# Attention stage of a two-layer diffusion block: row maxima in pairs, row sums by matmuls with ones, shift rows by one transposing matmul and DMA

## The chip, the cores and the metric

One core of one Trainium2 chip. The metric is the device time of one execution in microseconds; for each kernel the median of several runs is given.

## The reference

Two layers over 1024 latent and 256 context tokens of width 1024. Each layer projects the tokens into the features of three token mixers (grouped-query attention with 8 heads, latent attention with 4 heads, a gated linear recurrence), joins their outputs in one projection, and then runs a squared-ReLU MLP. The change touches only the softmax attention:

```python
s = jnp.einsum('bqhgd,bkhd->bhgqk', qi, k, preferred_element_type=F32) * scale
p = jax.nn.softmax(s, axis=-1).astype(v.dtype)
return jnp.einsum('bhgqk,bkhv->bqhgv', p, v)
```

Latent queries see all 1280 keys. Context queries see only the 256 context keys, and they are wanted in layer 0 alone.

## The kernel before, in words

The kernel is a row of stages (blocks), each of which ends with a barrier. `attention` (L1227) runs once in each layer, with the output projection behind it.

**Units and steps.** A unit is 512 queries of a pair of heads (`par` 0 and 1). A long unit goes over 10 key tiles of 128 keys in 10 steps; a short one (context queries, 2 steps) stands behind every fourth long one in layer 0. Layer 0 has 12 long and 3 short units (126 steps), layer 1 has 12 long ones (120 steps): 27 units in all. The first 8 long units of a layer belong to the grouped-query heads (called A here, tiles at_qq, at_qs, at_kk, at_ks, aq, av), the last 4 to the latent heads (B here, tiles qb, kb, bv).

**One step** on TensorE (`scores`, L1556): K·Q into a PSUM tile at_sT with the keys on the partitions, by 4 matmuls of 512 columns in A (2 per head, for the high and the low halves of the numbers) and 6 in B. ScalarE then takes exp of the 128x1024 tile (L1445) into a ring of PRING = 4 SBUF tiles at_p. Two steps later (LAG = 2) TensorE multiplies the values with at_p (`weighted`, L1568, fp32, the two heads into different halves of the output partitions) into at_acc, and GpSimd adds up at_p into at_accp (L1409, L1414: 9 additions in a long unit).

**Three small things** are needed around a unit, and all go through a ring of two one-bank PSUM tiles `sm` (at_small), in the order of one list, `small`. Task j writes sm[j % 2]; before it TensorE waits in `released` until task j - 2 has been read.
- *max*: the softmax shift must be known before the unit starts. So scores of 128 queries against up to 512 keys are computed once more with the queries on the partitions (L1511 in A, where the two heads use different halves of the input rows; L1515 in B), and VectorE takes the maximum along the row (L1465). A long unit has 24 of them (4 query tiles, key chunks of 512, 512 and 256, 2 heads), a short one 8. After the last of a unit VectorE combines the chunks (L1469) and negates (L1471).
- *row*: the shifts must be a row beside the query features, since the key side has a row of ones there. For each head four fp32 matmuls with one column of at_neg as weights and the identity moving (L1526, 16 instruction records per unit) make the row in PSUM, and ScalarE writes it to partition 64 of at_qs or 96 of qb (L1431).
- *sum* and *bc*: 8 fp32 matmuls with 128x128 of at_accp as weights and one column of ones moving (L1532, 16 records) give the row sums of a unit, VectorE takes 8 reciprocals per partition (L1475), and 8 fp32 matmuls against the identity (L1539, 16 records) spread them over the output layout. VectorE copies that to SBUF (L1480) and multiplies at_acc with it (L1483); ScalarE and GpSimd write the high and the low half of the result (L1436, L1397).

**Order.** `plan` lays the tasks out by step: the maxima of the next unit in the 8 first steps of a unit (3 per step), its rows in step 9, sum and bc 4 and 6 steps behind the unit's end. In each step TensorE runs `scores(i)`, the first EARLY = 2 tasks of the step, `weighted(i - 2)`, and then the step's other tasks. The maxima and rows of unit 0 run ahead of the loop. The loads of all query and key copies stand in SP's queue (L1376): 48 DMAs in layer 0 and 30 in layer 1 ahead of the loop, and those of the fourth head pair later.

Of the kernel before, what the change touches and what calls it, by code (L numbers as in the profile page):

```python
# [1203 lines left out]
EARLY = 2  # L1204
PRING = 4
# [21 lines left out]
def attention(nc, e, sem, l, f):  # L1227
# [60 lines left out]
    def released(eng, j):  # L1288
# [4 lines left out]
        elif kind == "row":  # L1293
            eng.wait_ge(s_row, rows_at[j])
        elif kind == "sum":
            eng.wait_ge(s_rc, u + 1)
        else:
            eng.wait_ge(s_bcast, u + 1)

    with ExitStack() as st:  # L1300
# [6 lines left out]
        mx, neg = sb("mx", [P, U, 2, 4, 3]), sb("neg", [P, U, 2, 4])  # L1307
        rc, o32 = sb("rc", [P, 2, 8]), sb("o32", [P, 2, 512])
# [5 lines left out]
        (s_ones, s_small, s_max, s_neg, s_row, s_S, s_p, s_pacc, s_pv, s_rc, s_bcast, s_read, s_hi, s_lo, s_d) = (  # L1314
            sem(nm + x) for x in (
                "ones_set", "small_done", "max_read", "shift_ready", "row_written", "scores_done", "exp_done",
                "added_by_pool", "pv_done", "reciprocals", "broadcast_read",
                "values_scaled", "hi_out", "lo_out", "dve"))

        per_pair = 16 * 6 * (2 if full else 1)  # L1320
        last_max, rows_at, rows_through = {}, {}, {}
# [785 lines left out]
```

## Time and profile before

| | us |
|---|---|
| median of 3 runs (lowest to highest) | 4673.59 (4664.94 to 4674.07) |
| the profiled execution's own time | 4658.89 |
| its span | 4657.1 |
| TensorE busy | 3890.6 (84%) |
| VectorE busy | 2161.6 (46%) |
| ScalarE busy | 1202.4 (26%) |
| GpSimd busy | 722.5 (16%) |

How it is read: the span is one execution on the core, cut by stages that follow each other; the table's shares are averages over all of them. TensorE's busy time is modelled and matmuls overlap, so a TensorE that shows as busy isn't thereby at its peak; what an instruction costs in a dense stretch is the distance from its start to the start of the next. A row of the trace has the start, the duration, the engine, the line, what is written and read with its shape, and the count of what was merged; in brackets the idle time before it and who ended it. A row of a stretch (the first group below) has the stretch, its length, then busy us and instructions of TensorE's matmuls, its weight loads, VectorE, ScalarE and GpSimd, the granted TensorE clock as a share of 2.4 GHz, the DMA share and GB/s.

### The profile page before, as it was taken

Reading aid. Unit: us, or ns where it says so; the run is one execution under the profiler, and the core shown is the slowest. Engines: PE = TensorE matmul, PEld = TensorE weight load, DVE = VectorE, ACT = ScalarE, POOL = GpSimd, SP = SyncE. Lnnn points to the kernel's source line nnn. Section 1 sums busy time; section 2 is a strip of 40 time slices with the busy share of each in tenths; the row PEclk is TensorE's granted clock in tenths of the full one; section 3 lists DMA queues with packets and bytes.
Section 4 is the critical chain, followed back from the end, with each engine's and each line's share of the span. In section 5 each row is a group of like instructions: output and inputs, shape, how many; then the busy total and the mean of one; then the engine's idle time right before and its main releaser. Section 6 shows DMA issues by size and latency. Waiting matters only on the chain. (4 is left out here: it accounts for less than half of the span.)

```text
span 4657.1 us, 49370 instructions
## 1 busy us (share of the span) xinstructions
PE 3890.6 (84%) x20550; PEld 2102.0 (45%) x20550; DVE 2161.6 (46%) x3601; ACT 1202.4 (26%) x1589; POOL 722.5 (16%) x412
## 2 busy tenths in 40 slices
PE   7698347789998889999997696359699985999996
PEld 6455235523334545555553454347233332444443
DVE  2781666555541443333334783665555405333334
ACT  1321224323331321111112221232233313221221
POOL 0000320036670000000000000310177600000000
PEclk7898665579998789999998797665699987999998
DMA  4110003110002211111100210022100021111110
GB/s 171 46 40 1 1 1 128 45 34 9 1 1 82 72 55 41 41 44 41 40 31 36 55 40 0 1 84 77 40 8 1 1 73 41 50 53 52 50 46 36
DMA packets 207632, 194.37 MB, mean 42 GB/s; under 512 B 9719, under 2 KB 174386, under 8 KB 206770
## 3 DMA queue, kind: packets, MB, share of 16 engines
q1 hardware_dynamic: 203250, 182.84, 12.6%
q10 hardware_dynamic: 4160, 8.39, 0.5%
q8 instruction: 162, 2.65, 0.2%
q14 instruction: 60, 0.49, 0.0%
HBM read 167.48 MB, written 14.68 MB: 39 GB/s over the span
## 5 line engine op out<-in xcount | busy, mean ns | idle before, releaser
L324 PE MATMUL mlp_acc<-hh,mlp_w 128*128 128x512 f16 (+1 forms) x3840 | 753.8, 359 | 52.9 <-DVE mlp_w L314 52.9
L324 PE MATMUL mlp_acc<-mlp_aa,mlp_w 128*128 128x512 f16 (+1 forms) x3840 | 749.2, 358 | 0.0
L324 PEld LDWEIGHTS mlp_acc<-hh,mlp_w 128*128 128x128 f16 x3840 | 376.7, 98 | 428.1 <-DVE mlp_w L314 53.8
L324 PEld LDWEIGHTS mlp_acc<-mlp_aa,mlp_w 128*128 128x128 f16 x3840 | 375.8, 98 | 371.1
L1465 DVE TENSOR_REDUCE at_mx<-at_small 128x1 f32<-128x512 f32 (+1 forms) x600 | 336.6, 591 | 320.2 <-PE at_small L1511 189.7
L1414 POOL TENSOR_TENSOR at_accp<-at_accp,at_p 128x1024 f32<-128x1024 f32 x192 | 450.6, 2347 | 143.9 <-ACT at_p L1445 142.5
L324 PE MATMUL in_acc<-hh,in_w 128*128 128x512 f16 (+1 forms) x2088 | 400.7, 355 | 70.1 <-DVE in_w L314 57.6
L1445 ACT ACTIVATE at_p<-at_sT 128x1024 f32<-128x1024 f32 x246 | 251.8, 1024 | 467.2 <-PE at_sT L1556 444.6
L647 DVE SCALAR_TENSOR_TENSOR yf<-mlp_acc,yf 128x1280 f32<-128x1280 f32 (+1 forms) x112 | 152.0, 1357 | 398.6 <-PE mlp_acc L324 398.6
L324 PEld LDWEIGHTS in_acc<-hh,in_w 128*128 128x128 f16 (+1 forms) x2088 | 208.3, 100 | 260.6 <-DVE in_w L314 58.4
L1851 PE MATMUL ro_sc<-hh 64*128 64x128 f32 x1008 | 104.7, 376 | 256.4 <-ACT ro_A L1739 142.2
L634 DVE TENSOR_TENSOR mlp_r<-mlp_r 128x1280 f32<-128x1280 f32 (+1 forms) x64 | 87.0, 1359 | 477.1 <-ACT mlp_r L615 477.1
L308 ACT ACTIVATE mlp_w<-mlp_stage 128x1024 f16<-128x1024 f32 x128 | 132.6, 1046 | 417.9 <-PE mlp_acc L324 404.0
L615 ACT ACTIVATE mlp_r<-mlp_acc 128x1280 f32<-128x1280 f32 (+1 forms) x64 | 72.3, 1130 | 640.7 <-PE mlp_acc L324 640.7
L324 PE MATMUL out_acc<-hh,out_w 128*128 128x512 f16 (+1 forms) x960 | 191.1, 363 | 36.2 <-DVE out_w L314 36.2
L98 PEld LDWEIGHTS pa_ada<-cact,pa_wada 128*128 128x128 f32 x1024 | 206.0, 307 | 27.5 <-issue 24.4
L1851 PEld LDWEIGHTS ro_sc<-hh 64*128 64x128 f32 x1008 | 93.1, 275 | 266.6 <-ACT ro_A L1739 144.9
L467 POOL MEMSET cc<- 128x40 f32 x2 | 0.3, 172 | 1346.0 <-POOLq L2066 1189.7
L98 PE MATMUL pa_ada<-cact,pa_wada 128*128 128x2 f32 x1024 | 199.9, 330 | 0.0
L1568 PE MATMUL at_acc<-at_p,av 128*64 128x512 f32 (+1 forms) x672 | 186.9, 638 | 0.3 <-DVE at_o L1483 0.3
L1722 POOL TENSOR_TENSOR hh<-cc,ro_val 128x256 f32<-128x256 f32 x126 | 134.8, 1102 | 327.6 <-DVE ro_ks L1780 327.6
L314 DVE SCALAR_TENSOR_TENSOR mlp_w<-mlp_stage,mlp_w 128x1024 f16<-128x1024 f32 x128 | 155.8, 1218 | 13.5 <-ACT mlp_w L308 13.5
(261 smaller groups left out, 4786.4 us busy)
## 6 DMA issues: line engine op xcount, KB each, us to landing
mlp_stage<-in_w_ff SPq DMA_DIRECT2D x128, 512.0 KB, 3.8
pa_wada<-in_w_ada SPq DMA_DIRECT2D x16, 2048.0 KB, 8.2
in_stage<-in_w_in SPq DMA_DIRECT2D x36, 512.0 KB, 4.4
set_wada<-in_w_ada ACTq DMA_DIRECT2D x4, 2048.0 KB, 19.4
out_stage<-in_w_out SPq DMA_DIRECT2D x16, 512.0 KB, 5.2
nf_wada<-in_w_ada SPq DMA_DIRECT2D x4, 2048.0 KB, 8.8
x<-x_scratch SPq DMA_DIRECT2D x1, 5120.0 KB, 15.9
xin<-in_x SPq DMA_DIRECT2D x8, 512.0 KB, 6.0
```

Of the source, the lines that this page charges most:

```text
L98: last = self.nc.tensor.matmul(self.acc[:, 4 * (self.first + j) + m, :], self.w[:, j % self.ring, k, m * P:(m + 1) * P], self.e.cact[:, k, :],
L308: self.nc.scalar.activation(self.w[:, r, 0, 0:size], self.stage[:, r, 0:size], ACT.Copy, scale=WSCALE)\
L314: self.nc.vector.scalar_tensor_tensor(self.w[:, r, 1, 0:size], self.stage[:, r, 0:size], WSCALE, self.w[:, r, 0, 0:size], ALU.mult, ALU.su ...
L324: last = self.nc.tensor.matmul(acc[0:mw, a:a + c], w[:, wh, k, m0:m0 + mw], src[:, sh, k0 + k, a:a + c], start=(k == 0 and wh == 0 and sh ...
L634: nc.vector.tensor_tensor(r[:, 0:ntok], r[:, 0:ntok], r[:, 0:ntok], ALU.mult).then_inc(s_sq, 1)
L647: nc.vector.scalar_tensor_tensor(y[:, j, 0:ntok], L.ps[i % 2][:, 0:ntok], 1.0 / (WSCALE * ASCALE), y[:, j, 0:ntok], ALU.mult, ALU.add)\
L1414: nc.gpsimd.tensor_tensor(to, to, p32[:, i % PRING, :, :], ALU.add).then_inc(s_pacc, 1)
L1445: nc.scalar.activation(p32[:, i % PRING, :, :], sT[i % 2][:, :, :], ACT.Exp).then_inc(s_p, 1)
L1465: nc.vector.reduce_max(mx[:, u, par, q, c:c + 1], sm[j % 2][:, 0:cks[c][1]], AX.X)\
L1568: last = nc.tensor.matmul(acc[u % 2][64 * par:64 * par + 64, c:c + n], value(pr, par, kts[s]), p32[:, i % PRING, par, c:c + n], start=(s = ...
L1722: last = nc.gpsimd.tensor_tensor(half(X[b % 2][:, :, i, :], h, 0), mid(b, h), half(val[:, b % 2, :, :], h, 0), ALU.subtract)
L1851: last = nc.tensor.matmul(to, keys, queries, start=True, stop=True)
```

## The change

- The maxima of a long unit become 20 tasks: 16 of one query tile against 512 keys, and 4 in which two query tiles against the last 256 keys share one PSUM tile, so that one reduction reads 512 columns for both. A short unit has 4. They are laid out as a stream of pairs (both heads), one pair per step, that ends LEAD = 4 steps ahead of the unit; in the first three steps of a layer there are two pairs per step.
- All tasks of a step now run between `scores(i)` and `weighted(i - 2)`.
- The shifts (at_neg, now fp16, 8 columns) become rows by one matmul with a 128x128 fp16 identity, ScalarE copies 8x128 values to SBUF, and SP's queue moves them to partition 64 or 96 by DMA: 2 per long unit, 4 per short one, behind all the loads ahead of the loop. The row task is 3 steps ahead of its unit.
- The sums become 2 fp32 matmuls with 64 columns of ones as weights and 512 columns of at_accp moving, which leaves each sum on all 64 partitions of its head. The spreading matmuls (bc) are gone. ScalarE copies the sums to SBUF; VectorE takes the reciprocal of 128x512 values in four pieces of 128 columns, one per step, and multiplies 8 steps behind the unit's end. In front of a short unit, and at the end of a layer, all four pieces and the product come in one step.
- The ring at_p has 5 tiles.

```diff
 LAG = 2
-EARLY = 2
-PRING = 4
+PRING = 5
+LEAD = 4
 QRING = 3
...
     def maxes(u):
-        return [("max", u, par, q, c) for q in range(4) for c in range(len(units[u].keys)) for par in range(2)]
+
+        if not units[u].long:
+            return [("max", u, par, 0, (q, q + 1)) for q in (0, 2) for par in range(2)]
+        whole = [("max", u, par, c, (q,)) for q in range(4) for c in range(2) for par in range(2)]
+        return whole + [("max", u, par, 2, (q, q + 1)) for q in (0, 2) for par in range(2)]
+
+    sum_at, piece_at, scale_at = {}, {}, {}
...
-        first = [t for t in maxes(0)] + [("row", 0, par) for par in range(2)]
-        for k, u in enumerate(long):
-            nxt = list(range(u + 1, long[k + 1] + 1)) if k + 1 < len(long) else list(range(u + 1, U))
-            todo = [t for v in nxt for t in maxes(v)]
-            for s in range(8):
-                take = -(-len(todo) // (8 - s))
-                want.setdefault(base[u] + s, []).extend(todo[:take])
-                todo = todo[take:]
-            want.setdefault(base[u] + 9, []).extend(("row", v, par) for v in nxt for par in range(2))
+        for t in maxes(0) + [("row", 0)]:
+            want.setdefault(-1, []).append(t)
+        both = [(u, k) for u in range(1, U) for k in range(len(maxes(u)) // 2)]
+        when = {}
+        for n in range(len(both) - 1, -1, -1):
+            u, k = both[n]
+            when[n] = min(base[u] - LEAD, when.get(n + 1, N) - (1 if n + 1 < len(both) else 0))
+        for n, (u, k) in enumerate(both):
+            want.setdefault(max(when[n], n // 2), []).extend(maxes(u)[2 * k:2 * k + 2])
+        for u in range(1, U):
+            want.setdefault(base[u] - LEAD + 1, []).append(("row", u))
         for u in range(U):
             end = base[u + 1] - 1
             soon = u + 1 < U and not units[u + 1].long
-            want.setdefault(end + (3 if soon else 4), []).append(("sum", u))
-            want.setdefault(end + (4 if soon else 6), []).append(("bc", u))
-        for t in first:
-            put(-1, t)
+            sum_at[u] = min(end + 3, N)
+            want.setdefault(sum_at[u], []).append(("sum", u))
+            for k in range(4):
+                piece_at.setdefault(min(end + (4 if soon else 4 + k), N), []).append((u, k))
+            scale_at[u] = min(end + (4 if soon else 8), N)
         for i in sorted(want):
             for t in want[i]:
-                put(min(i, N), t)
+                put(i, t)
...
         elif kind == "row":
-            eng.wait_ge(s_row, rows_at[j])
-        elif kind == "sum":
-            eng.wait_ge(s_rc, u + 1)
+            eng.wait_ge(s_row, u + 1)
...
-        mx, neg = sb("mx", [P, U, 2, 4, 3]), sb("neg", [P, U, 2, 4])
-        rc, o32 = sb("rc", [P, 2, 8]), sb("o32", [P, 2, 512])
+        mx, top = sb("mx", [P, U, 2, 4, 3]), sb("top", [P, 8])
+        neg, ident = sb("neg", [P, U, 8], F16), sb("ident16", [P, P], F16)
+        row = sb("row", [8, 2, P], F16)
+        o32 = sb("o32", [P, 2, 512])
...
+        def shifts(u):
+            return sum(16 * 2 * len(units[v].parts) for v in range(u % 2, u + 1, 2))
...
-                for pr in range(4):
+                def load(pr):
...
-                    if pr >= QRING:
-                        sp.wait_ge(s_S, base[last_use[pr - QRING] + 1])
...
+                for pr in range(QRING):
+                    load(pr)
+                for u in range(U):
+                    sp.wait_ge(s_row, u + 1)
+                    for par in range(2):
+                        for pr, tok, c, n in units[u].parts:
+                            r = 4 * par + c // P
+                            dst = shift_row(pr, par)[:, tok:tok + n]
+                            sp.dma_start(dst, row[r:r + n // P, u % 2, :]).then_inc(s_shift[u % 2], 16)
+                    if u == last_use[0] + 1:
+                        sp.wait_ge(s_S, base[last_use[0] + 1])
+                        load(QRING)
...
-                    while done < U and base[done + 1] + 8 <= i:
+                    while done < U and scale_at[done] + 2 <= i:
...
-                            for pr, tok, c, n in units[u].parts:
-                                row, R = shift_row(pr, small[j][2])
-                                nc.scalar.activation(row[:, tok:tok + n], sm[j % 2][R:R + 1, c:c + n], ACT.Copy)\
-                                  .then_inc(s_row, 1)
+                            nc.scalar.activation(row[:, u % 2, :], sm[j % 2][0:8, 0:P], ACT.Copy).then_inc(s_row, 1)
+                        elif kind == "sum":
+                            act.wait_ge(s_small, j + 1)
+                            if u >= 2:
+                                act.wait_ge(s_lo, u - 1)
+                            nc.scalar.activation(o32[:, u % 2, :], sm[j % 2][:, :], ACT.Copy).then_inc(s_sums, 1)
...
-                    while done < U and base[done + 1] + 7 <= i:
+                    while done < U and scale_at[done] + 1 <= i:
...
+                tasks(N)
...
-                            nc.vector.reduce_max(mx[:, u, par, q, c:c + 1], sm[j % 2][:, 0:cks[c][1]], AX.X)\
+                            nc.vector.reduce_max(mx[:, u, par, qs_[0]:qs_[-1] + 1, c],
+                                                 sm[j % 2][:, 0:w * len(qs_)].rearrange("p (q n) -> p q n", n=w), AX.X)\
...
-                                ch(nc.vector.reduce_max(neg[:, u, :, :], mx[:, u, :, :, 0:len(cks)], AX.X))
+                                if u:
+                                    dve.wait_ge(s_neg, u)
+                                ch(nc.vector.reduce_max(top[:, :].rearrange("p (a q) -> p a q", a=2),
+                                                        mx[:, u, :, :, 0:len(units[u].keys)], AX.X))
                                 ch.wait(dve)
-                                nc.vector.tensor_scalar(neg[:, u, :, :], neg[:, u, :, :], -1.0, MSHIFT,
-                                                        ALU.mult, ALU.add).then_inc(s_neg, 1)
-                        elif kind == "sum":
-                            dve.wait_ge(s_small, j + 1)
-                            nc.vector.reciprocal(rc[:, u % 2, :], sm[j % 2][:, 0:8]).then_inc(s_rc, 1)
-                        elif kind == "bc":
-                            dve.wait_ge(s_small, j + 1)
-                            if u >= 2:
-                                dve.wait_ge(s_lo, u - 1)
-                            nc.vector.tensor_copy(o32[:, u % 2, :], sm[j % 2][:, :]).then_inc(s_bcast, 1)
-                            dve.wait_ge(s_bcast, u + 1)
+                                nc.vector.tensor_scalar(neg[:, u, :], top[:, :], -1.0, MSHIFT, ALU.mult, ALU.add)\
+                                  .then_inc(s_neg, 1)
+
+                pieces = {}
+
+                def scale(i):
+                    for u, k in piece_at.get(i, []):
+                        part = o32[:, u % 2, k * P:(k + 1) * P]
+                        dve.wait_ge(s_sums, u + 1)
+                        pieces[u] = ch(nc.vector.reciprocal(part, part))
+                    for u in range(U):
+                        if scale_at[u] == i:
                             dve.wait_ge(s_pv, base[u + 1])
+                            ch.wait(dve, pieces[u])
                             nc.vector.tensor_tensor(o32[:, u % 2, :], o32[:, u % 2, :], acc[u % 2][:, :], ALU.mult)\
                               .then_inc(s_read, 1)
 
...
+                nc.vector.tensor_copy(ident[:, :], e.ident[:, :]).then_inc(s_id, 1)
...
+                            for n, q in enumerate(tiles):
...
+                                last = nc.tensor.matmul(out[:, n * w:(n + 1) * w], query, key, start=True, stop=True)
...
-                            par = small[j][2]
                             pe.wait_ge(s_neg, u + 1)
-                            for q in range(4):
-                                pr, _ = units[u].tile(q)
-                                if pr < 4 and (pr, "q") not in loaded:
-                                    pe.wait_ge(s_load[pr % QRING], per_pair * (pr // QRING + 1))
-                                    loaded.add((pr, "q"))
-                                R = shift_row(pr, par)[1]
-                                last = nc.tensor.matmul(out[R:R + 1, q * P:(q + 1) * P], neg[:, u, par, q:q + 1],
-                                                        e.ident[:, :], start=True, stop=True)
-                        elif kind == "sum":
+                            if u == 0:
+                                pe.wait_ge(s_id, 1)
+                            last = nc.tensor.matmul(out[0:8, 0:P], neg[:, u, :], ident[:, :], start=True, stop=True)
+                        else:
                             pe.wait_ge(s_pacc, adds_p[base[u + 1] - 1])
                             for par in range(2):
-                                for q in range(4):
-                                    last = nc.tensor.matmul(out[:, 4 * par + q:4 * par + q + 1],
-                                                            accp[:, u % 2, par, q * P:(q + 1) * P], e.ones[:, 0:1],
-                                                            start=True, stop=True)
-                        else:
-                            pe.wait_ge(s_rc, u + 1)
-                            for q in range(4):
-                                for par in range(2):
-                                    last = nc.tensor.matmul(out[64 * par:64 * par + 64, q * P:(q + 1) * P],
-                                                            rc[:, u % 2, 4 * par + q:4 * par + q + 1].broadcast_to([P, 64]),
-                                                            e.ident[:, :], start=True, stop=True)
+                                last = nc.tensor.matmul(out[64 * par:64 * par + 64, :], e.ones[:, 0:64],
+                                                        accp[:, u % 2, par, :], start=True, stop=True)
...
-                        pe.wait_ge(s_row, rows_through[u])
+                        pe.wait_ge(s_shift[u % 2], shifts(u))
+                        for pr, _, _, _ in units[u].parts:
+                            if pr < 4 and (pr, "q") not in loaded:
+                                pe.wait_ge(s_load[pr % QRING], per_pair * (pr // QRING + 1))
+                                loaded.add((pr, "q"))
...
-                    tasks(i, slice(0, EARLY))
+                    tasks(i)
                     if i >= LAG:
                         weighted(i - LAG)
-                    tasks(i, slice(EARLY, None))
```

## Rows read from the trace of the kernel before

**Rows 1.** Busy time by stretch: the two attention loops, and one unit of A

```profile
997.30:1414.00 416.70, 406.77 (x2136) 160.83 (x2136) 201.38 (x361) 153.77 (x175) 276.74 (x126) 0.95 0.02 5
3360.00:3740.00 380.00, 372.26 (x1864) 137.12 (x1864) 185.76 (x322) 142.22 (x154) 266.44 (x120) 0.96 0.01 3
...
3452.10:3482.80 30.70, 30.70 (x153) 10.64 (x152) 16.72 (x29) 11.93 (x13) 22.17 (x11) 0.94 0.01 1
```

**Rows 2.** Timeline of TensorE in A, layer 1, 3453 to 3466 us

```profile
3453.50 0.39 PE L1511 MATMUL at_small<-at_kk,aq 64*128 64x512 f16 x1
3453.82 0.39 PE L1556 MATMUL at_sT<-at_qq,at_kk 128*128 128x512 f16 x1
...
3454.79 0.39 PE L1511 MATMUL at_small<-at_kk,aq 64*128 64x512 f16 x2
3455.11 1.08 PE L1568 MATMUL at_acc<-at_p,av 128*64 128x512 f32 x4
3456.12 0.28 PE L1511 MATMUL at_small<-at_kk,aq 64*128 64x256 f16 x1
3456.33 1.95 PE L1532 MATMUL at_small<-ones,at_accp 128*128 128x1 f32 x16
3458.14 0.38 PE L1556 MATMUL at_sT<-at_qq,at_kk 128*128 128x512 f16 x1
...
3459.64 1.97 PE L1568 MATMUL at_acc<-at_p,av 128*64 128x512 f32 x4
...
3464.79 1.09 PE L1539 MATMUL at_small<-ident,at_rc 128*64 128x128 f32 x16
```

**Rows 3.** Timeline of TensorE in B, layer 1

```profile
3656.38 1.47 PE L1556 MATMUL at_sT<-qb,kb 97*128 97x512 f16 x6
3657.69 0.49 PE L1515 MATMUL at_small<-kb,qb 96*128 96x512 f16 x2
3658.10 1.08 PE L1568 MATMUL at_acc<-at_p,bv 128*64 128x512 f32 x4
...
3663.05 1.91 PE L1526 MATMUL at_small<-ident,at_neg 128*1 128x128 f32 x16
```

**Rows 4.** Groups by line and shape, whole span: busy us, mean ns

```profile
L391 DVE RECIPROCAL in_t<-in_t 128x640 f32<-128x640 f32 x24 | 99.7, 4153 | 0.8
...
L1532 PE MATMUL at_small<-ones,at_accp 128*128 128x1 f32 x432 | 55.0, 257 | 3.4 <-POOL at_accp L1414 2.0 <-DVE at_mx L1465 1.4
...
L1471 DVE TENSOR_SCALAR at_neg<-at_neg 128x8 f32<-128x8 f32 x27 | 31.7, 1174 | 0.9
...
L391 DVE RECIPROCAL in_t<-in_t 128x512 f32<-128x512 f32 x8 | 26.8, 3353 | 0.3
```

**Rows 5.** Timeline of layer 1's step 1: two maxima, and the third behind them

```profile
3363.51 0.39 PE L1511 MATMUL at_small<-at_kk,aq 64*128 64x512 f16 x2
...
3364.68 0.28 PE L1511 MATMUL at_small<-at_kk,aq 64*128 64x256 f16 x1 [0.79 <-DVE at_mx L1465]
```

**Rows 6.** Timeline around a negation of the shifts, GpSimd beside it

```profile
3380.05 2.35 POOL L1414 TENSOR_TENSOR at_accp<-at_accp,at_p 128x1024 f32<-128x1024 f32 x1 [0.28 <-ACT at_p L1445]
...
3380.88 0.18 DVE L1469 TENSOR_REDUCE at_neg<-at_mx 128x8 f32<-128x24 f32 x1
...
3381.10 1.34 DVE L1471 TENSOR_SCALAR at_neg<-at_neg 128x8 f32<-128x8 f32 x1
```

**Rows 7.** TensorE's first scores of each layer, from timelines of TensorE

```profile
997.34 0.61 PE L1556 MATMUL at_sT<-at_qq,at_kk 128*128 128x512 f16 x1 [0.68 <-ACT at_qs L1431]
...
3360.05 0.40 PE L1556 MATMUL at_sT<-at_qq,at_kk 128*128 128x512 f16 x1 [0.68 <-ACT at_qs L1431]
```

**Rows 8.** SP's last load ahead of the loop, layers 0 and 1

```profile
1002.67 0.60 SPq L1376 DMA_DIRECT2D at_qs<-aq  x1
...
3354.72 0.62 SPq L1376 DMA_DIRECT2D at_qs<-aq  x1
```

**Rows 9.** DMA issues by line: KB each, median us from issue to landing

```profile
at_qs<-aq SPq DMA_DIRECT2D x8, 32.0 KB, 1.9
```

More of the change, by code:

```diff
@@ L1313, in attention @@
         s_kload = [sem(f"{nm}keys_loaded{i}") for i in range(2)]
-        (s_ones, s_small, s_max, s_neg, s_row, s_S, s_p, s_pacc, s_pv, s_rc, s_bcast, s_read, s_hi, s_lo, s_d) = (
+        s_shift = [sem(f"{nm}shift_rows_in{i}") for i in range(2)]
+        (s_ones, s_id, s_small, s_max, s_neg, s_row, s_S, s_p, s_pacc, s_pv, s_sums, s_read, s_hi, s_lo, s_d) = (
             sem(nm + x) for x in (
-                "ones_set", "small_done", "max_read", "shift_ready", "row_written", "scores_done", "exp_done",
-                "added_by_pool", "pv_done", "reciprocals", "broadcast_read",
-                "values_scaled", "hi_out", "lo_out", "dve"))
+                "ones_set", "identity_ready", "small_done", "max_read", "shift_ready", "row_written", "scores_done",
+                "exp_done", "added_by_pool", "pv_done", "sums_copied", "values_scaled", "hi_out", "lo_out", "dve"))
         per_pair = 16 * 6 * (2 if full else 1)
-        last_max, rows_at, rows_through = {}, {}, {}
+        last_max = {}
         for j, t in enumerate(small):
@@ L1324, in attention @@
                 last_max[t[1]] = kinds[:j + 1].count("max")
-            elif t[0] == "row":
-                rows_at[j] = sum(len(units[w[1]].parts) for w in small[:j + 1] if w[0] == "row")
-                rows_through[t[1]] = rows_at[j]
+        def shifts(u):
+            return sum(16 * 2 * len(units[v].parts) for v in range(u % 2, u + 1, 2))
         def hi_of(t, q):
@@ L1343, in shift_row @@
         def shift_row(pr, par):
-            return (qs[64:65, pr % QRING, par, :], 64) if pr < 4 else (f.qb[96:97, 0, 2 * (pr - 4) + par, :], 96)
+            return qs[64:65, pr % QRING, par, :] if pr < 4 else f.qb[96:97, 0, 2 * (pr - 4) + par, :]
         def value(pr, par, kt):
@@ L1407, in _ @@
                             if u >= 2:
-                                pool.wait_ge(s_rc, u - 1)
+                                pool.wait_ge(s_sums, u - 1)
                             nc.gpsimd.tensor_tensor(to, p32[:, (i - 1) % PRING, :, :], p32[:, i % PRING, :, :],
@@ L1488, in _ @@
                     tasks(i)
-                tasks(N)
+                    scale(i)
+                scale(N)
             @block.tensor
@@ L1493, in _, with tasks @@
                 loaded = set()
-                def tasks(i, part=slice(None)):
-                    for j in at.get(i, [])[part]:
+                def tasks(i):
+                    for j in at.get(i, []):
                         kind, u = small[j][0:2]
@@ L1501, in tasks @@
                         if kind == "max":
-                            _, _, par, q, c = small[j]
-                            pr, tok = units[u].tile(q)
-                            if pr < 4 and pr % 2 == 0 and pr not in loaded:
-                                pe.wait_ge(s_kload[pr // 2], 16 * 6)
-                                loaded.add(pr)
+                            _, _, par, c, tiles = small[j]
                             a, w = units[u].keys[c]
                             a += units[u].kts[0] * P
-                            if pr < 4:
-                                R = slice(64 * par, 64 * par + 64)
-                                last = nc.tensor.matmul(out[:, 0:w], hi_of(f.aq[R, pr, :], tok),
-                                                        kk[R, pr // 2, a:a + w], start=True, stop=True)
-                            else:
-                                b = 2 * (pr - 4) + par
-                                last = nc.tensor.matmul(out[:, 0:w], f.qb[0:96, 0, b, tok:tok + P],
-                                                        f.kb[0:96, 0, b, a:a + w], start=True, stop=True)
+                            for n, q in enumerate(tiles):
+                                pr, tok = units[u].tile(q)
+                                if pr < 4 and pr % 2 == 0 and pr not in loaded:
+                                    pe.wait_ge(s_kload[pr // 2], 16 * 6)
+                                    loaded.add(pr)
+                                if pr < 4:
+                                    R = slice(64 * par, 64 * par + 64)
+                                    query, key = hi_of(f.aq[R, pr, :], tok), kk[R, pr // 2, a:a + w]
+                                else:
+                                    b = 2 * (pr - 4) + par
+                                    query, key = f.qb[0:96, 0, b, tok:tok + P], f.kb[0:96, 0, b, a:a + w]
+                                last = nc.tensor.matmul(out[:, n * w:(n + 1) * w], query, key, start=True, stop=True)
```

8 lines of the change are left out of this document (4 added, 4 removed).

## The prediction

> **What bounds the kernel now.** I read the stretches first. In both attention loops, 417 and 380 us long, TensorE is busy for 98% of the time, GpSimd for 66 to 70%, VectorE for about half and ScalarE for 37% [rows 1]. So TensorE's own instructions set the pace, and what is taken off it there comes out of the time as long as nobody else becomes the bound. One unit of A lasts 30.7 us; GpSimd works 22.2 of it [rows 1], so the unit can't fall below that by this change.
>
> Then the timeline of TensorE, start to start. In A, scores take 3454.79 - 3453.82 = 0.97 us and the value product 3456.12 - 3455.11 = 1.01; two maxima of both heads side by side take 0.32, a single one of 512 columns 0.32 as well, one of 256 columns 0.21; a sum task takes 1.81 and a bc task 1.09 [rows 2]. In B scores take 1.31 and a pair of maxima 0.41; a row task takes 1.91 [rows 3]. Ten steps of 1.98, 4.6 of maxima (eight steps of 0.32 plus on average 0.26), 1.91 + 1.81 + 1.09 for the three small tasks make 29.2 of the 30.7 us. The rest is the clock: 0.94 in this unit [rows 1] is 30.7 x 0.06 = 1.8 us lost at 1.2 GHz. It is seen in the value product behind the sum, which takes 1.97 where the one before took 1.08 [rows 2]. No idle time stands ahead of it, only 16 instructions with one moving column each. The trace has 11 such falls in the two loops, each behind a sum task: 7 in layer 1, and 4 in layer 0, two of them twice as long. At 1.8 us for each single one that is 13 x 1.8 = 23 us; the clock columns of both loops (0.95 and 0.96) allow 36 in all, their slow starts and ends among them [rows 1]. I take 22.
>
> **The change, part by part.** All times are against the profiled execution (4658.9 us, 14.7 under the median of 4673.6).
>
> *Sums, bc and rows.* Each of 27 units (432 records of 16 [rows 4]) loses 1.81 + 1.09 + 1.91 = 4.81 us and gets two products of the shape of the value product, 1.01 [rows 2], and one fp16 matmul of 128 columns. The latter has no row; it is shorter than the 0.21 of 256 columns [rows 2] and more than nothing; I take 0.15. Net 3.65 x 27 = 98.5; the first row task of each layer runs ahead of the loop and is counted there, so -95.
>
> *Maxima.* A long unit of A goes from 4.6 to 10 pairs of 0.32 = 3.2, so 1.4 less for 14 units: -20. In B, eight steps of 0.41 plus 0.18 become ten pairs of 0.41, so 0.6 less for 8 units: -5. Three short units have half the tasks: about -1 each, -3. Together -28.
>
> *New stalls.* The ring has two tiles, a pair fills both, and nothing of `weighted` stands between the pair and a row or sum task of the same step any more. What this costs the trace shows in step 1 of a layer, where `weighted` is missing too: the third task starts 3364.68 - 3363.51 = 1.17 us behind the pair, held by VectorE's first maximum [rows 5]. A pair takes 0.32, so a sum task waits 0.85 in A and 0.76 in B: 15 and 7 of them, 18 us. (Five sums have no maxima beside them.) A row task comes one step behind the last pair of its unit, and VectorE is late there: both maxima are read 1.17 + 0.69 = 1.86 us behind that pair, the combination takes 0.2, and the negation 1.17 on average [rows 4], since it ends where GpSimd's addition ends (3381.10 + 1.34 = 3382.44 beside 3380.05 + 2.35 = 3382.40) while the combination just before it takes its 0.18 undisturbed [rows 6]. That is 3.3 us; the next pair's first maximum is read 0.7 later, at 4.0, where TensorE, one step of 2.3 us on, is done with that pair at 2.6. So a row task waits 1.4 us in A (18 of them) and 0.9 in B (4): 29 us. In the first three steps two pairs per step stand in the same way, 0.69 more for each further task: +3 per layer, 6. Together +53, between 22 (if every wait were the least, 0.5) and 60.
>
> *Reciprocals.* 512 columns took 3.35 and 640 took 4.15 us, 6.25 ns per column [rows 4], so a piece of 128 takes 0.95. In such a step of A VectorE needs 2 x 0.69 + 0.95 + gaps = 2.45 against TensorE's 0.97 + 0.32 + 1.01 = 2.30. The lag of 0.15 in each of four steps uses up a reserve of 2.30 - 1.86 = 0.44; +3 over all units, at most 0.6 x 15 = 9. The product with at_acc and the copies (ScalarE has 60% of its time free [rows 1]) are covered.
>
> *GpSimd's additions* stay at 9 x 2.35 and 1.16 per unit; TensorE's unit becomes 19.8 + 3.2 + 1.2 + 2.3 of stalls = 26.5 us in A, above 22.2. The fifth tile of at_p only loosens this; nothing for it.
>
> *Shift rows by SP.* Inside the loop: the row task ends about 1.9 us into its step, ScalarE's copy 0.3 later, then two issues of 0.64 and a landing 1.9 us behind the last issue [rows 9], so 4.8 us, and the unit's first scores come about 7.4 us into it. Hidden, with 2.6 to spare. Ahead of the loop it is not. SP's queue issues loads until 1002.67 + 0.60 in layer 0 [rows 8]; the two shift DMAs go at 1003.3 and 1003.9 and land at 1005.8, where scores began at 997.34 [rows 7]: +8.5. In layer 1 the queue is free at 3355.3 [rows 8], about when the shifts are ready, so scores begin near 3358.2, 1.8 earlier than 3360.05 [rows 7], but behind an idle gap, at 1.2 GHz for some us: 0.
>
> *Ends of the layers.* The last sum is 0.8 cheaper and bc is gone, but four pieces (3.8 us) follow; layer 0 has eight. +2 in all.
>
> *Clock.* The one-column instructions that precede every fall are gone. What comes in their place are waits of 0.85 and 1.4 us. Steps 0 and 1 of layer 1 have two waits of 0.8 us close together (the second in [rows 5]) and stay at full clock, so I take the falls as gone: -22.
>
> Sum: -95 - 28 + 53 + 3 + 8.5 + 0 + 2 - 22 = -78; I take -74, since some clock falls will be met by chance. 4673.6 - 74 = 4599.6.
>
> **The rivals.**
>
> *The clock falls stay.* The waits are still time in which TensorE does nothing, and they come in each unit, 0.85 in one step and 1.4 in another. Against it: rows 5. Then the -22 is missing: -52, 4622. The Trainium skill (TensorE: Matmul & The Clock Gate, HAM oscillation) ties the fall to TensorE's idle gaps; by that rule the new waits are what matters and the one-column matmuls, which leave no gap, are innocent. The trace doesn't agree: its falls stand behind the sums without any idle time.
>
> *The reciprocals are held by GpSimd*, as the negation is, whose mean is 1.17 where it takes 0.17 alone. Before, the reciprocal read PSUM; now it reads and writes SBUF, as the negation does. Each piece then waits 1.0 us more: VectorE needs 3.45 us in a step of 2.30, TensorE waits 4 x 1.15 - 0.44 = 4.2 instead of 0.2 in 15 units of A, and 4 x 0.72 - 0.44 = 2.4 in 7 of B, together +77, and with such waits the falls of the clock stay: -52 + 77 = +25, 4699. This is the case in which the change makes it slower. It decides from a hold of 0.7 us per piece on. Against it: the combination reads and writes SBUF just before the negation and is never held [rows 6], and a reciprocal takes six times a plain pass anyway. The Trainium skill (GPSIMD Engine Reference, Specifications) names as rivals of GpSimd those VectorE instructions that run in a two-port mode or have two SBUF inputs, and its table in VectorE: DVE Perf Modes gives that mode to copies and scalar operations; rows 6 agree for the negation, and no row tells it for a reciprocal.
>
> *The shift rows are late in the loop*, when a landing takes over 4.5 us or SP stands in its wait for the fourth pair's buffers (12 DMAs, 8 us, with 16 us until the next row). 25 units by 1 to 2 us: -74 + 38 = -36, 4638. The median landing of a small one is 1.9 us [rows 9].
>
> *The waits are much smaller*, because the reordered tasks let VectorE run ahead: +53 becomes +25, 4572.
>
> **Chances and range.** Forecast 0.55; clock falls stay 0.2; waits smaller 0.06; rows late 0.04; reciprocals held 0.08; another wait that I don't see, about +30 on the forecast, 0.07. The range for 8 in 10 reaches from -105 (small waits, the lower bound of their cost) to -28 (falls stay, upper bounds of stalls and reciprocals): 4569 to 4646. A measurement of this kernel can tell about 0.2% (9 us, the spread of its three runs). Faster by more than that 0.88, within it 0.05, slower 0.07.
>
> **What would show it.** In the changed profile: L1532's place taken by 54 matmuls of 512 columns, about 1.0 us a pair; at_neg with 8 weight columns once per unit; the unit of A near 26 us; TensorE's idle time in the loops up from 8 to 10 us each to some 25 to 30, ended by VectorE's maximum, ahead of sum and row tasks; reciprocals of 0.95 us; first scores of layer 0 at about 1006; clock 1.00 inside the units of A. I am wrong if reciprocals take 2 us, if scores wait for DMA inside the loop, if GpSimd gets above 95% busy in A, or if the clock column stays at 0.94.

## The result, and the profile after

The changed kernel takes 4643.97 us (median of 5 runs, 4632.93 to 4659.56) against 4673.59 (5 runs, 4664.05 to 4683.27): ratio 0.9942, 95% interval 0.9913 to 0.9970. It is faster by some 30 us, where 74 were forecast and 4569 to 4646 was the range; the number lies at its very edge, and less than half of the forecast gain came. The profiled execution took 4638.12 us, span 4636.3, so 20.8 less than that of before (4658.89).

Busy time by stretch, changed kernel (columns as in [rows 1]): the loops of layer 0 and 1 from first to last scores, then one unit of A in layer 1.

```profile
997.80:1379.40 381.60, 341.77 (x1480) 100.57 (x1482) 227.23 (x325) 146.32 (x166) 272.73 (x123) 0.94 0.01 3
3336.30:3705.20 368.90, 334.72 (x1349) 92.25 (x1349) 208.05 (x297) 137.24 (x152) 261.12 (x117) 0.91 0.01 3
...
3421.10:3451.80 30.70, 27.17 (x110) 6.79 (x109) 18.97 (x28) 11.63 (x13) 22.25 (x11) 0.89 0.00 1
```

The same stretches of the kernel before, cut from first to last scores as well:

```profile
997.30:1398.40 401.10, 395.54 (x2054) 151.74 (x2056) 198.20 (x355) 151.49 (x172) 272.08 (x123) 0.96 0.02 5
3360.00:3726.50 366.50, 364.88 (x1822) 132.20 (x1824) 184.17 (x319) 140.56 (x152) 260.72 (x117) 0.97 0.01 3
```

Layer 0's loop is 19.5 us shorter, layer 1's 2.4 us longer, and a unit of A lasts 30.7 us, exactly as before. TensorE's work did shrink: 84 us less busy time in the two loops. But it now stands still in them for 74 us instead of 7, and its clock, the column behind the busy times, went down instead of up. What the lower clock costs is the length of a stretch times what the column lacks to 1.00: 27 us before (0.04 x 401 + 0.03 x 367) and 56 after (0.06 x 382 + 0.09 x 369). In the unit of A the column fell from 0.94 to 0.89; that it would stay at 0.94 was the prediction's sign of being wrong.

Who TensorE waits for in the attention stages, whole span (us in total, times, longest):

```profile
PE at_small L1552 <- DVE at_mx L1488: 48.6, 24, 2.8
...
PE at_small L1556 <- DVE at_mx L1488: 20.6, 22, 3.7
...
PE at_sT L1576 <- DMA at_qs<-at_row: 16.0, 2, 13.2
...
PE at_small L1547 <- DVE at_mx L1488: 9.2, 24, 0.8
```

L1552 is the row task, L1556 the sum. The row tasks cost 48.6 us, a mean of 2.0, where I had 1.4 in A and 0.9 in B. The two waits for the shift rows' DMA are those ahead of the loops; inside the loops there is none. The timeline of one such row task (three engines):

```profile
3418.00 7.19 POOL L1434 TENSOR_TENSOR at_accp<-at_accp,at_p 128x1024 f32<-128x1024 f32 x3
...
3420.54 0.18 DVE L1495 TENSOR_REDUCE at_top<-at_mx 128x8 f32<-128x24 f32 x1
...
3420.76 2.04 DVE L1498 TENSOR_SCALAR at_neg<-at_top 128x8 f16<-128x8 f32 x1
...
3421.11 0.39 PE L1547 MATMUL at_small<-at_kk,aq 64*128 64x512 f16 x2
...
3422.71 0.94 DVE L1507 RECIPROCAL at_o<-at_o 128x128 f32<-128x128 f32 x1
3423.57 1.21 DVE L1488 TENSOR_REDUCE at_mx<-at_small 128x1 f32<-128x512 f32 x2
3424.25 0.27 PE L1552 MATMUL at_small<-at_ident,at_neg 128*8 128x128 f16 x1 [2.75 <-DVE at_mx L1488]
3424.45 1.98 PE L1588 MATMUL at_acc<-at_p,av 128*64 128x512 f32 x4
...
3428.71 1.98 PE L1588 MATMUL at_acc<-at_p,av 128*64 128x512 f32 x4
...
3431.95 0.65 PE L1588 MATMUL at_acc<-at_p,av 128*64 128x512 f32 x2
```

VectorE's queue is what counts here. The pair of maxima that TensorE wrote at 3421.11 is read only behind the negation, which is held until GpSimd's addition ends (three additions of 2.4 from 3418.00 on, so the second ends at 3422.8, and so does the negation: 3420.76 + 2.04), and behind the fourth reciprocal piece, which the schedule puts in just this step. TensorE stands still for 2.75 us, and behind that two whole steps run at 1.2 GHz (value products of 1.98). In layer 1 such a pair of slow steps stands behind each of the six row waits of 2.7 us in A. In both layers together 12 waits of 2.6 us or more are followed by 11 falls, some of them of one step only in layer 0; three more falls stand behind row waits of 1.74 to 1.95.

The two new VectorE operations, by group (busy us, mean ns):

```profile
L1507 DVE RECIPROCAL at_o<-at_o 128x128 f32<-128x128 f32 x108 | 99.1, 933 | 55.1 <-ACT at_o L1454 55.1
...
L1498 DVE TENSOR_SCALAR at_neg<-at_top 128x8 f16<-128x8 f32 x27 | 46.2, 1709 | 0.9
```

A reciprocal takes 0.89 to 0.95 whether GpSimd works or not (it did beside 92 of the 108). The negation now takes 1.71 on average against 1.17 in [rows 4]. Ahead of layer 0's loop, from the timelines of SP and TensorE:

```profile
995.40 1.35 SPq L1408 DMA_DIRECT2D at_qs<-at_row  x2
...
997.81 0.61 PE L1576 MATMUL at_sT<-at_qq,at_kk 128*128 128x512 f16 x1 [13.22 <-DMA at_qs<-at_row]
```

The stage began with SP's first load at 964.10, so its first scores come 33.7 us into it, against 25.4 before (971.93 and [rows 7]).

### The profile page after: what moved, and what is told of

Its sections match the earlier page's. It is cut to its first block and busy times, and to the rows that moved or that the text cites. A ratio compares the mean times of both kernels' runs of the same rounds, so it can differ in the third digit from the quotient of the medians.

```text
span 4636.3 us, 47025 instructions
## 1 busy us (share of the span) xinstructions
PE 3783.9 (82%) x19389; PEld 1990.3 (43%) x19389; DVE 2224.6 (48%) x3549; ACT 1194.1 (26%) x1583; POOL 723.6 (16%) x412
## 5 line engine op out<-in xcount | busy, mean ns | idle before, releaser
L1488 DVE TENSOR_REDUCE at_mx<-at_small 128x1 f32<-128x512 f32 (+1 forms) x492 | 315.7, 683 | 293.3 <-PE at_small L1547 290.7
```

Source lines behind the costliest of these rows:

```text
L1488: nc.vector.reduce_max(mx[:, u, par, qs_[0]:qs_[-1] + 1, c], sm[j % 2][:, 0:w * len(qs_)].rearrange("p (q n) -> p q n", n=w), AX.X)\
```

## The experiments

Theory 1: the waits ahead of row and sum tasks and the clock falls behind the long ones ate the gain. Theory 2: the clock falls from the dense work itself, whatever the waits. Theory 3: GpSimd, 22.2 us busy per unit of A, is the next bound. All ratios below are to the kernel before, run beside each experiment; the changed kernel stands at 0.9942.

**Row and sum tasks behind the value product** (a_late)

```diff
-                def tasks(i):
+                def tasks(i, late=None):
                     for j in at.get(i, []):
                         kind, u = small[j][0:2]
                         out = sm[j % 2]
+                        if late is not None and late != (kind != "max"):
+                            continue
...
-                    tasks(i)
+                    tasks(i, False)
                     if i >= LAG:
                         weighted(i - LAG)
+                    tasks(i, True)
```

> The changed kernel with one edit: row and sum tasks run behind the value product of their step, the pair of maxima stays ahead of it. Theory 1 (TensorE's waits ahead of row and sum tasks, 2.75 and 0.78 us in a unit of A, and the clock falls of two steps behind the long ones eat the gain): the sum's wait goes, the row's falls to about 1.7, and if that is short enough for the clock, a unit of A goes from 30.7 to about 26 us and the time from 4644 to about 4570; if the clock still falls, to about 4605. Theory 2 (the falls come from the dense work itself, not from waits): waits shrink but the clock column of layer 1's loop stays at 0.91, time about 4605. Theory 3 (GpSimd is the next bound): GpSimd above 90% busy in A and the time stays within 15 us of 4644.

4594.34 us, ratio 0.984 (0.9824 to 0.9855). No sum task waits any more, a row task in A waits 1.75 instead of 2.75, and a unit of A takes 27.5 us (row tasks at 3400.8 and 3428.3). Two waits in layer 0 only moved: beside its short units the value product now waits, for 3.24 and 2.49 us. The clock column of layer 1's loop is 0.94: one slow step per unit of A instead of two. So the order alone brings about 47 us, between the two numbers of theory 1.

**The fourth reciprocal piece one step later** (b_piece)

```diff
-                piece_at.setdefault(min(end + (4 if soon else 4 + k), N), []).append((u, k))
+                piece_at.setdefault(min(end + (4 if soon else (4, 5, 6, 8)[k]), N), []).append((u, k))
```

> The changed kernel with the fourth reciprocal piece moved from the row task's forerunner step (7 behind the unit's end) to the step of the product (8 behind it). Theory 1: the row's wait in A falls from 2.75 by the 0.94 of one piece to 1.8, 17 units: -16 us, and -45 to -60 if the clock no longer falls behind it. Theory 2: -16 at most, clock column of layer 1's loop unchanged at 0.91.

4610.19 us, ratio 0.9868 (0.985 to 0.9885). The row's wait in A is 1.95, one piece shorter. The unit of A takes 27.0 us instead of 30.7: 0.8 of that is the wait, the other 2.9 the clock, whose column in layer 1 went from 0.91 to 0.96. One placement of a 0.94 us operation was worth 34 us.

**No held negation** (c_neg)

```diff
-                            nc.scalar.activation(row[:, u % 2, :], sm[j % 2][0:8, 0:P], ACT.Copy).then_inc(s_row, 1)
+                            nc.scalar.activation(row[:, u % 2, :], sm[j % 2][0:8, 0:P], ACT.Copy, bias=MSHIFT).then_inc(s_row, 1)
...
-                                ch(nc.vector.reduce_max(top[:, :].rearrange("p (a q) -> p a q", a=2),
-                                                        mx[:, u, :, :, 0:len(units[u].keys)], AX.X))
-                                ch.wait(dve)
-                                nc.vector.tensor_scalar(neg[:, u, :], top[:, :], -1.0, MSHIFT, ALU.mult, ALU.add)\
-                                  .then_inc(s_neg, 1)
+                                nc.vector.reduce_max(neg[:, u, :].rearrange("p (a q) -> p a q", a=2),
+                                                     mx[:, u, :, :, 0:len(units[u].keys)], AX.X).then_inc(s_neg, 1)
...
-                nc.vector.tensor_copy(ident[:, :], e.ident[:, :]).then_inc(s_id, 1)
+                nc.vector.tensor_scalar(ident[:, :], e.ident[:, :], -1.0, None, ALU.mult).then_inc(s_id, 1)
```

> The changed kernel without the negation on VectorE (held up to 2.04 us by GpSimd's addition): the combination writes fp16 directly, the identity of the transposing matmul is negative, and ScalarE adds the constant in its copy. Theory 1: the row's wait in A falls from 2.75 to about 1.1, 22 rows: -35 us, and if the clock falls go with it, -75, to about 4570. Theory 2: -35, clock column 0.91 as before. That the hold is no cost (VectorE would be late anyway): under -10.

4588.12 us, ratio 0.982 (0.9804 to 0.9837). The same step as above, in this kernel's timeline:

```profile
3409.57 0.18 DVE L1495 TENSOR_REDUCE at_neg<-at_mx 128x8 f16<-128x24 f32 x1
...
3409.67 0.94 DVE L1504 RECIPROCAL at_o<-at_o 128x128 f32<-128x128 f32 x1
...
3410.14 0.39 PE L1544 MATMUL at_small<-at_kk,aq 64*128 64x512 f16 x2
...
3410.56 1.29 DVE L1488 TENSOR_REDUCE at_mx<-at_small 128x1 f32<-128x512 f32 x2
3411.31 0.22 PE L1549 MATMUL at_small<-at_ident,at_neg 128*8 128x128 f16 x1 [0.78 <-DVE at_mx L1488]
3411.46 1.08 PE L1585 MATMUL at_acc<-at_p,av 128*64 128x512 f32 x4
```

The row waits 0.78, the same as a sum, with the fourth piece still in its step, and the value product behind it runs at full clock. In layer 1 no fall is left in the loop behind its first steps. One 8-column instruction, of whose 2.04 us all but 0.17 are the hold, was the largest single loss: 57 us with the falls that hung on it. (The gains of the three edits don't add up: all of them act on the same wait.) Theory 2 has fallen: the work is the same and denser, and in layer 1 the clock stays up.

**All three** (abc)

> All three edits together. Theory 1: hardly a wait of TensorE for VectorE in the units of A, unit of A near 24.5 us (20 of scores and products, 3.2 of maxima, 1.2 of sum and row), clock 1.00 inside them, time about 4560. Theory 2: clock falls remain inside the units of A without any idle time ahead of them, time about 4590 to 4600. Theory 3: GpSimd at 90% or more in A and ScalarE waiting for it, unit of A between 24.5 and 27.

4547.87 us, ratio 0.9741 (0.9726 to 0.9757), 124 us below the kernel before (4671.87). One unit of A, by stretch:

```profile
3398.30:3422.40 24.10, 24.10 (x112) 6.38 (x110) 17.11 (x27) 11.63 (x13) 22.32 (x11) 1.00 0.00 1
```

24.1 us at full clock, TensorE without a gap in this unit. GpSimd works for 22.3 of them, 93%, yet ScalarE never waits for it inside the loops: theory 3 doesn't hold here; that GpSimd would be the next bound follows from the 93% and was not run. The whole of both loops:

```profile
1008.40:1347.90 339.50, 331.42 (x1480) 99.08 (x1482) 204.47 (x311) 146.23 (x165) 273.16 (x123) 0.97 0.02 4
3298.90:3612.20 313.30, 310.92 (x1349) 89.02 (x1351) 188.38 (x286) 137.28 (x152) 261.74 (x117) 0.97 0.01 3
```

The slow steps left are those at the loops' starts and two in layer 0. These two stand behind the long waits beside the short units, where four pieces and the product come in one step:

```profile
1127.48 1.98 PE L1587 MATMUL at_acc<-at_p,av 128*64 128x512 f32 x4 [3.24 <-DVE at_o L1509]
```

The other wait is 2.49 us. In the changed kernel and in all its variants each of these two waits (3.75 and 3.00 where the sum task still has them) has a fall behind it.

**Unit 0's shift rows ahead of the third pair's loads** (abc_front, on top of the three)

```diff
-                for pr in range(QRING):
-                    load(pr)
+                load(0)
+                load(1)
                 for u in range(U):
...
+                    if u == 0:
+                        load(2)
```

> The three edits, and SP issues the shift rows of unit 0 behind the loads of the first two head pairs instead of three; the third pair's loads follow. If the 13 us between the maxima's end and the first scores of layer 0 are the queue of loads and nothing else, layer 0's first scores come 8 to 9 us earlier after the stage's start (33.7 us in the kernel with the three edits) and layer 1's about 2 (23.1): 4548 goes to about 4538. If the landing of the small DMA is what takes the time, no change.

4541.85 us, ratio 0.9732 (0.9712 to 0.9753). The interval is too wide to tell 10 us from 0, but the stage's start shows it. SP's first load and TensorE's first scores of layer 0:

```profile
980.08 1.33 SPq L1385 DMA_DIRECT2D at_kk<-ak  x2
...
1000.70 1.36 SPq L1408 DMA_DIRECT2D at_qs<-at_row  x2
```

```profile
1003.11 0.61 PE L1577 MATMUL at_sT<-at_qq,at_kk 128*128 128x512 f16 x1 [2.74 <-DMA at_qs<-at_row]
```

23.0 us instead of 33.7, and TensorE's wait ahead of them is 2.74 instead of 13.4: the queue of loads was all of the rest, and the shift rows now go when they are ready. In layer 1 nothing moved (23.1), since the 30 loads there were nearly out anyway; I had expected 2 us.

**One-column matmuls put back** (abc_onecol, on top of the three)

```diff
                             pe.wait_ge(s_pacc, adds_p[base[u + 1] - 1])
+                            for q in range(8):
+                                nc.tensor.matmul(out[:, q:q + 1], accp[:, u % 2, q // 4, q % 4 * P:(q % 4 + 1) * P],
+                                                 e.ones[:, 0:1], start=True, stop=True)
```

> The three edits, with the 8 one-column fp32 matmuls (16 records) of the old sum put back ahead of each sum, as dead work. By length alone 27 x 1.8 = 49 us: 4548 to 4597. If such matmuls bring the clock down by themselves, as read from the kernel before, a fall follows in most units of A, 1.8 us each, some 11 to 13 of them: about 4618, clock column of layer 1's loop down from 0.97 to 0.93. If the falls of the kernel before had another cause: 4597 and 0.97.

4624.06 us, ratio 0.9916 (0.9899 to 0.9932): 82 us more by the ratios (0.0175 x 4670), where 49 is their length. The stretches of its two loops:

```profile
1009.42:1389.85 380.43, 372.34 (x1688) 126.95 (x1690) 204.44 (x311) 146.21 (x165) 272.99 (x123) 0.93 0.01 3
3347.58:3688.00 340.42, 338.06 (x1525) 109.83 (x1527) 188.34 (x286) 137.17 (x152) 261.53 (x117) 0.96 0.01 3
```

With the three edits alone the column had 0.97 in both, so some 20 us are clock. The two loops are 68 us longer, the length and the clock; the other 14 by the ratios lie outside them and are not explained. But the falls don't come where I expected them: the units of A in layer 1 stay at full clock (24.1 us becomes 26.1, the length alone), and of the new slow steps all but one stand in units of B or beside the short units. So one-column matmuls do not bring the clock down wherever they stand.

**The kernel before with dense sums** (before_dense)

```diff
-                                for q in range(4):
-                                    last = nc.tensor.matmul(out[:, 4 * par + q:4 * par + q + 1],
-                                                            accp[:, u % 2, par, q * P:(q + 1) * P], e.ones[:, 0:1],
-                                                            start=True, stop=True)
+                                last = nc.tensor.matmul(out[64 * par:64 * par + 64, :], e.ones[:, 0:64],
+                                                        accp[:, u % 2, par, :], start=True, stop=True)
```

> The kernel before, with the 8 one-column matmuls of each sum replaced by the two dense ones with ones as weights; the reciprocals then read numbers that aren't the sums in their place, so the output's scale is left out of the computation, with every instruction as before. By length 27 x 0.8 = 22 us less than before. If the one-column matmuls bring the clock down: 45 us less, and no falls inside the units of A (clock column of layer 1's loop from 0.97 to 0.99). If the falls come from something else: 22 less and 7 falls in layer 1 as before.

This kernel leaves out the scale of the output; every other instruction is as before. 4611.44 us, ratio 0.9899 (0.9878 to 0.992), 47 us less by the ratio where 22 is the length. One unit of A:

```profile
3422.20:3450.60 28.40, 28.40 (x143) 8.88 (x142) 16.71 (x29) 11.95 (x13) 22.21 (x11) 1.00 0.00 1
```

28.4 us instead of 30.7, clock 1.00 instead of 0.94, and none of the 11 falls inside the loops is left; the loop columns are 0.99 and 0.98. So in the kernel before the falls did hang on the one-column matmuls. With the run above, that is as much as is shown: they are followed by falls in one schedule (behind 11 of the 24 sums inside the loops) and hardly at all in A of another, and what makes the difference was not tried.

**Two checks of sizes.** The ring of at_p back at 4 tiles (abc_ring4; `PRING = 5` to `PRING = 4`), and the three edits without the moved piece (ac_only; `(4, 5, 6, 8)[k]` back to `4 + k`):

> The three edits with the ring of exponentials at 4 tiles as in the kernel before. GpSimd is busy for 22.3 of the 24.1 us of a unit of A there, its additions run up to 5 in a row behind the exponentials. If the ring's fifth tile is what lets them lag, ScalarE waits for GpSimd with 4 tiles and the time rises from 4548 by 10 to 25 us; if the lag never reaches four tiles (what the prediction took), no change (within 5).

> The two edits on the order (row and sum tasks behind the value product) and on the negation, with the four reciprocal pieces where the change put them. Theory 1, by sizes: once the held negation is gone, VectorE is late by one piece of 0.94 only, which the value product's 1.01 covers, so the same time as with all three edits, 4548 within 5. If the piece still makes TensorE wait: 4 to 15 more.

4549.35 us, ratio 0.9741 (0.9702 to 0.978), and 4546.32, ratio 0.9732 (0.9699 to 0.9766). Neither differs from the three edits. The fifth tile brings nothing here. And of the three edits two are enough: once the held negation is gone the piece costs nothing (in c_neg too the row waits 0.78 with the piece in its step).

## Why the prediction was wrong, step by step

**The removed and added work was nearly right.** It was put at -95 and -28. With all three edits, where next to nothing waits, TensorE's busy time in the two loops is 118 us less than before; some 8 of that is the clock (27 us lost before, 20 with the edits), so the work is some 110 less, where 123 were forecast. The whole kernel is 124 us below the kernel before. The reciprocals (0.95 forecast, 0.93 measured on average) were not held by GpSimd; that rival is out. So is the late shift row in the loop: TensorE never waited for its DMA there.

**The first step that failed is the size of the row task's wait.** I put it at 1.4 us in A. In most units of A it was 2.75, for two reasons that both could be read beforehand. First, I took the negation at its mean, 1.17, over 27 instructions that also held undisturbed ones; in the new schedule GpSimd's additions run back to back beside it and it took 2.03 to 2.05 in seven units of A in layer 1. An instruction that waits for a neighbour's next end has no price of its own; it has to be placed in the new order. Second, I costed the reciprocal pieces against the average step and the row wait without them, and did not see that the fourth piece (7 steps behind the end of unit u) and the last maxima of unit u + 2 (4 steps ahead of it) are the same step. The two add up in VectorE's queue. Row and sum waits together were forecast at 47 us and measured at 69. In layer 0 the sum tasks of the two short units that have maxima beside them waited 3.75 and 3.00, since the four pieces and the product of the unit in front come in one step; these I had priced like all others.

**The second step that failed, and the larger one, is the clock term: it got the wrong sign.** It was put at -22, for falls that would be gone. That the one-column matmuls cost the clock in the kernel before was right (before_dense: 47 us, of which 22 are length). But I took the new waits as harmless, on the strength of two waits of 0.8 in a layer's first steps. At 2.75 they weren't: the clock took 56 us in the two loops instead of 27, and not 5. The rival that the falls stay was the nearest to what came, at too small a price.

Not all of the 29 us more belong to the waits. Some 11 stand at the loops' starts, nearly 3 of them in layer 0. Layer 1's loop began at half clock for its first 15.9 us, 8 us lost, and the profiled execution of the kernel before happened to begin it at full clock (1.00 in 3360.05:3376.00). The changed kernel, and before_dense, whose way into the loop is the old one:

```profile
3336.30:3352.20 15.90, 13.55 (x31) 2.92 (x32) 7.73 (x12) 3.07 (x3) 4.68 (x2) 0.50 0.00 0
```

```profile
3323.60:3339.50 15.90, 14.34 (x39) 3.30 (x40) 6.85 (x12) 4.10 (x4) 5.47 (x3) 0.57 0.00 1
```

A slow start comes without the change too, so these 8 us are not shown to be its cost. The falls inside the loops are the rest: some 18 us more, on top of the 22 that were to go; without the long row waits layer 1's are gone (c_neg).

With the measured terms the two loops close as follows. TensorE's busy time is 84 us less although the clock adds about 29 to it, so the work is about 113 less; the time in which it stands still is 67 more (74 against 7); the clock takes 29 more. That makes -17, and the loops are 17.1 us shorter (19.5 less, 2.4 more). The forecast for them was -123 + 53 + 3 - 22 = -89. So of the 72 us that are missing the clock is 51 and the largest part, the waits are 11, and the work 10. (Row and sum waits alone are 22 more than forecast; against that, the waits of the first steps came out smaller, the 3 for the pieces don't show apart, and a few small waits of before are gone.) The way into layer 0's loop is 8.3 longer (forecast 8.5), that of layer 1 is 2.2 shorter (forecast 0), and the ends are 2.4 shorter where I had 2 longer: from the last scores to GpSimd's last write 15.4 became 14.5 and 13.1 became 11.6. That is -13 for both attention stages. The other 7 us between the two profiled executions lie in stages whose code is the same: layer 0's attention began at 971.93 us before, at 964.10 here and at 980.08 in abc_front. The ratio of the medians gives 14 to 41 us, which the 13 of these two executions just misses; where the rest of the median's gain comes from is not shown.

**Whether a wait is followed by a fall isn't settled by its length.** In layer 1's A, waits of 1.75 behind the value product had a slow step behind each (a_late), waits of 1.8 to 2.0 ahead of it only two in seven (b_piece), waits of 0.78 none (c_neg). Nor does the length settle how long the fall is: behind 2.75 us two steps in layer 1, in layer 0 two, one or none. What decides between the first two was not tried and stays open.

## What to carry to other kernels

When a cheap instruction shows widely different durations, look at what it ends with: here an 8-column operation on VectorE ended with GpSimd's addition, and taking it off VectorE's queue brought 57 us of a 4.6 ms kernel. When tasks with a short ring are reordered, write out for the critical step everything that stands in the queue of the engine that frees the ring, in order, and not each piece against an average step. And keep work between producing into a small ring and needing it again: moving row and sum tasks behind the value product was a change of a few lines and 47 us.

## What the runs showed of the hardware that I had not expected

- A VectorE instruction can be held by GpSimd to the end of its running instruction, and others beside it aren't. In the changed kernel the 128x8 tensor_scalar took 0.17 us where GpSimd stood still and 0.6 to 2.05 beside an addition, and each of these 25 ended within 0.03 us of an addition's end; the 128x8 reduction took 0.16 to 0.18 and the 128x128 reciprocal 0.89 to 0.95, with GpSimd adding or not. All three read and write SBUF. The Trainium skill (GPSIMD Engine Reference, Specifications, and the tier table of VectorE: DVE Perf Modes) draws such a line by the two-port mode; the traces agree with it for the first two, and the table has no row for the reciprocal.
- TensorE's clock can fall without idle time: in the kernel before, 11 of the 24 sums inside the loops (16 one-column fp32 matmuls each) were followed by a fall, 10 of them with no gap ahead that is worth naming and one behind 0.78 us (clock column 0.94 in a unit of A), and none where two dense products of 1.01 us stand in their place (1.00). In abc_onecol the same matmuls in units of A of layer 1 had no fall behind them (1.00), so they are not enough by themselves. The rule of the Trainium skill (TensorE: Matmul & The Clock Gate, HAM oscillation) speaks of idle gaps, and of longer ones than any row wait, forecast or measured, in this case: it covers neither these falls nor those behind the waits of 2.75 us.
